# Low parts of a recurrent layer's input projection moved from GpSimd to VectorE, and its gates, scans, transposes and states made between weight blocks

## What is computed

```python
proj = h @ w_in                       # 1024 x 4096: q, fz, iv, g
q = silu(q);  v = iv
logf = log(lb + (1 - lb) * sigmoid(fz))
k = (1 - lb) * sigmoid(-fz)
b = cumsum(logf)                      # in chunks of 64 tokens; running sequences: of 4
scores = (q * exp(b - b_mid)) @ (k * exp(b_mid - b)).T     # causal, in the chunk
o = scores @ v + (q * exp(b)) @ S     # S: state at the chunk's start
S = exp(b_last) * S + (k * exp(b_last - b)).T @ v          # next chunk's state
out = (rmsnorm(o) * norm_w * silu(g)) @ w_out
```

## Time and profile before

| | us |
|---|---|
| median of 3 runs | 2119.61 |
| lowest and highest run | 2115.03, 2119.63 |
| span of the profiled execution | 2113.4 |
| from the first product of the projection to that of the head loop (1078.58 to 1219.45) | 140.9 |
| PE busy, whole span | 1857.5 |
| DVE, ACT, POOL busy, whole span | 1699.5, 1275.6, 588.8 |

### The profile page before, as it was taken

The page is one execution under the profiler, slowest core; times in us unless marked ns, Lnnn a source line. Parts: engine busy times, 40 slices in busy tenths (PEclk is TensorE's granted clock), DMA queues, the critical chain, the costliest instruction groups (busy, mean ns, idle before and its releaser), DMA issues. The chain is left out here.

```text
span 2113.4 us, 48775 instructions
## 1 busy us (share of the span) xinstructions
PE 1857.5 (88%) x17644; PEld 1607.3 (76%) x17644; DVE 1699.5 (80%) x3245; ACT 1275.6 (60%) x2621; POOL 588.8 (28%) x473
## 2 busy tenths in 40 slices
PE   1254889899999999999988877999999999999998
PEld 0243667788888888888866665778898898888887
DVE  8899568878889888879835596797889897887996
ACT  3532478666565556656578674886565655656554
POOL 6495057600000022213247501791000001221330
PEclk7555899999999999999999958999999999999999
DMA  2000334555556588889854204455555566888894
GB/s 89 26 1 2 125 111 151 164 185 177 173 178 206 172 290 299 304 271 331 311 202 146 90 11 179 141 168 181 173 182 173 173 211 220 300 300 278 313 331 163
DMA packets 107550, 396.30 MB, mean 188 GB/s; under 512 B 12976, under 2 KB 12976, under 8 KB 107056
## 3 DMA queue, kind: packets, MB, share of 16 engines
q1 hardware_dynamic: 88416, 318.37, 42.8%
q0 software_dynamic: 19024, 76.59, 11.8%
HBM read 388.72 MB, written 6.19 MB: 187 GB/s over the span
## 5 line engine op out<-in xcount | busy, mean ns | idle before, releaser
L229 ACT ACTIVATE wsp<-ring 128x512 f16<-128x512 f32 x1200 | 749.4, 629 | 627.4 <-PE ps L292 599.0
L290 PE MATMUL ps<-hs,wsp 128*128 128x256 f16 (+1 forms) x2672 | 737.9, 276 | 43.6 <-POOL wsp L240 31.5
L292 PE MATMUL ps<-hs,wsp 128*128 128x256 f16 (+1 forms) x2672 | 737.5, 276 | 0.0
L291 PE MATMUL ps<-hs,wsp 128*128 128x256 f16 (+1 forms) x2672 | 737.4, 276 | 0.0
L290 PE MATMUL ps<-hT,wsp 128*128 128x256 f16 x2048 | 559.1, 273 | 6.3 <-DVE hT L1791 6.3
L291 PE MATMUL ps<-hT,wsp 128*128 128x256 f16 x2048 | 559.0, 273 | 0.0
L292 PE MATMUL ps<-hT,wsp 128*128 128x256 f16 x2048 | 559.0, 273 | 0.0
L242 DVE SCALAR_TENSOR_TENSOR wsp<-ring,wsp 128x512 f16<-128x512 f32 x560 | 374.7, 690 | 134.3 <-ACT wsp L229 132.7
L249 DVE SCALAR_TENSOR_TENSOR wsp<-ring,wsp 128x1024 f16<-128x1024 f32 x216 | 264.2, 1224 | 102.9 <-ACT wsp L229 98.2
L290 PEld LDWEIGHTS ps<-hs,wsp 128*128 128x128 f16 x2672 | 261.6, 98 | 92.3 <-POOL wsp L240 34.0
L1550 POOL DMA_INDIRECT big<-in_rows,small x64 | 75.0, 1172 | 890.7 <-DVE small L1472 532.2
(11 more groups left out here) (299 smaller groups left out, 2110.2 us busy)
## 6 DMA issues: line engine op xcount, KB each, us to landing
ring<-in_v SPq DMA_DIRECT2D x256, 512.0 KB, 5.9
ring<-in_ub SPq DMA_DIRECT2D x216, 512.0 KB, 3.8
ring<-in_ua SPq DMA_DIRECT2D x40, 512.0 KB, 4.2
ring<-in_wq SPq DMA_DIRECT2D x32, 512.0 KB, 3.7
ring<-in_win SPq DMA_DIRECT2D x32, 512.0 KB, 3.7
ring<-in_glu SPq DMA_DIRECT2D x16, 512.0 KB, 4.3
big<-in_hgs POOLq DMA_DIRECT2D x1, 4096.0 KB, 13.3
ring<-in_wout SPq DMA_DIRECT2D x8, 512.0 KB, 3.9
```

The costliest lines, as they stand in the source:

```text
L229: nc.scalar.activation(wsp[:, k % 2, 0, cols], ring[:, k, cols], ACT.Copy, scale=scale).then_inc(hi_ready, 1)
L290: nc.tensor.matmul(out, w_hi, hi, start=start, stop=False, **kw)
L291: nc.tensor.matmul(out, w_hi, lo, start=False, stop=False, **kw)
L292: return nc.tensor.matmul(out, w_lo, hi, start=False, stop=stop, **kw)
```

## The change

1. "win" leaves `BY_POOL`: VectorE makes its low parts (line 242 in place of 240), the scaling pass of ScalarE is gone, GpSimd's loop over the 32 blocks too. The lows of block 0 are made at the end of peer_v_dve, those of block 1 in norm_dve between the rows of hT and their low parts.
2. The blocks come in the order fz, v, q, g. Q_ and D1 swap places in `big`. The first three heads of q are copied out and get their silu later in one operation.
3. The work on the gates is cut into pieces, each tied to a block number: a gate per head at blocks 1 to 8, two scans at each of 10 to 13, differences by half the heads at 14 to 17, products by half the heads at 19 to 25, 27 and 28. ScalarE's large activations stand at 8, 9, 14 and 16 to 19.
4. PE transposes the values behind blocks 23, 24, 25, the keys behind 25, 26, 27, and makes the chunk products behind 29, 30, 31. ScalarE copies the values out at blocks 24 to 26, VectorE the keys at 26 to 28; the chunk states stand right behind VectorE's loop, ahead of the masks.
5. The projection's trips are written out on PE (eight times four blocks) where a loop stood.
6. The lower bounds are worked out during the second pass of the expert layer ahead, at its blocks 66 and 71. Some semaphores of the expert layers are shared by both layers.

```diff
-BY_POOL = {"wq0", "ua0", "wq1", "ua1", "win"}
+BY_POOL = {"wq0", "ua0", "wq1", "ua1"}
...
+            if k == 2:
+                split_lo(v, "win", 0, 1)
             if before:
                 for c in range(KC):
                     low(c)
...
+                if L == 0 and b == 66:
+                    hg_lb_start_dve(v, cnt)
+                if L == 0 and b == 71:
+                    hg_lb_dve(v, cnt)
+            if L == 0:
+                split_lo(v, "win", 0, 0)
...
+        def hg_values_pe(pe, j):
+            pe.wait_ge(hg_ev, 16)
+            if j:
+                pe.wait_ge(hg_tvc, j)
+            hg_transpose_pe(pe, VT, 0, j, hg_tv)
+
+        def hg_keys_pe(pe, j):
+            pe.wait_ge(hg_m, 4)
+            if j:
+                pe.wait_ge(hg_tkc, j)
+            hg_transpose_pe(pe, KD, 2, j, hg_tk)
+
+        def hg_chunk_pe(pe, c):
+            pe.wait_ge(hg_tvc, 3)
+            pe.wait_ge(hg_tkc, 3)
+            if c >= 2:
+                pe.wait_ge(hg_S, c - 1)
...
         def hg_in_pe(pe):
-            project(pe, "win", lambda i, k, first: None if first else pe.wait_ge(hg_ev, i * 4 + k - 3),
-                    inputs=2)
+            def after(i, k, first):
+                b = i * RING + k
+                if 23 <= b < 26:
+                    hg_values_pe(pe, b - 23)
+                if 25 <= b < 28:
+                    hg_keys_pe(pe, b - 25)
+                if b >= 29:
+                    hg_chunk_pe(pe, b - 29)
+            for trip in range(8):
+                project(pe, "win", lambda i, k, first: None if first else pe.wait_ge(hg_ev, i * 4 + k - 3), after,
+                        trip, trip + 1, inputs=2)
+            hg_chunk_pe(pe, 3)
...
+            def between(b):
+                if b in (8, 9):
+                    heads_ = slice(4 * (b - 8), 4 * (b - 8) + 4)
+                    act.wait_ge(hg_f, 8 * (b - 7))
+                    nc.scalar.activation(h3(Bc)[:, heads_, :], h3(Bc)[:, heads_, :], ACT.Ln).then_inc(hg_log, 1)
+                elif b == 14:
+                    act.wait_ge(hg_cum, 8)
+                    nc.scalar.activation(QI, CU, ACT.Exp).then_inc(hg_e, 1)
+                elif b == 16:
+                    act.wait_ge(hg_d, 3)
+                    nc.scalar.activation(QM, D1, ACT.Exp).then_inc(hg_e, 1)
+                elif b == 17:
+                    nc.scalar.activation(KM, D1, ACT.Exp, scale=-1.0).then_inc(hg_e, 1)
+                elif b == 18:
+                    act.wait_ge(hg_d, 6)
+                    nc.scalar.activation(KD, Bc, ACT.Exp).then_inc(hg_e, 1)
+                elif b == 19:
+                    act.wait_ge(hg_ev, 16 + QUICK)
+                    nc.scalar.activation(h3(Q_)[:, 0:QUICK, :], h3(Q_)[:, 0:QUICK, :], ACT.Silu).then_inc(hg_e, 1)
+                elif 24 <= b < 27:
+                    hg_values_act(act, b - 24)
...
+            for b in range(32):
+                if b + 2 < 32:
+                    split_lo(v, "win", *divmod(b + 2, RING))
+                if 1 <= b < 9:
+                    gate(b - 1)
+                elif 10 <= b < 14:
+                    for h in (2 * (b - 10), 2 * (b - 10) + 1):
+                        scan(h)
...
+                if b in (24, 25):
+                    v.wait_ge(hg_ev, 24)
+                    v.wait_ge(hg_e, 5)
+                    times(QI, Q_, b - 24)
+                elif 26 <= b < 29:
+                    keys_out(b - 26)
+                if b in (27, 28):
+                    times(QM, Q_, b - 27)
...
+            for c in range(NCH):
+                state(c)
```

More of the change, by code:

```diff
@@ L1827, in h3 @@
             return a.rearrange("p (h t) -> p h t", h=HH)
-        Bc, K_, Q_, VT, GS, QM, QI, KM, KD, D1 = (unit(k) for k in range(10))
+        Bc, K_, D1, VT, GS, QM, QI, KM, KD, Q_ = (unit(k) for k in range(10))
         CU = bg(U * 10, U)
@@ L1856, in build @@
         lbr = sb("lbr", [P, 2, KC])
-        lb, oml = (small[:, 8 * k:8 * k + 8] for k in range(2))
-        lt = [small[:, 16 + 8 * k:24 + 8 * k] for k in range(4)]
+        lb, oml = (small[:, 200 + 8 * k:208 + 8 * k] for k in range(2))
+        lt = [small[:, 216 + 8 * k:224 + 8 * k] for k in range(4)]
         dec = small[:, 64:64 + 12 * HH].rearrange("p (h c) -> p h c", h=HH)
@@ new lines, in hg_values_pe @@
+        def hg_values_pe(pe, j):
[13 more added lines that the diff above has]
+                pe.wait_ge(hg_S, c - 1)
+            j, r0 = c // 2, CH * (c % 2)
+            for h in range(HH):
+                mm = nc.tensor.matmul(ps[:, 2 * (c % 2) + h // 4, (h % 4) * P:(h % 4 + 1) * P],
+                                      ktok[j][r0:r0 + CH, h * P:(h + 1) * P], vtok[j][r0:r0 + CH, h * P:(h + 1) * P],
+                                      start=True, stop=True)
+            mm.then_inc(hg_kv, 1)
@@ new lines, in build, with hg_evac_act @@
+        QUICK = 3
+        def hg_evac_act(act, b):
+            block_used(act, "win", *divmod(b, RING))
+            h = b % HH
+            if b < 8:
+                fns = [(Bc, ACT.Sigmoid, 1.0), (K_, ACT.Sigmoid, -1.0)]
+            elif b < 16:
+                fns = [(VT, ACT.Copy, 1.0)]
+            elif b < 24:
+                fns = [(Q_, ACT.Copy if h < QUICK else ACT.Silu, 1.0)]
+            else:
+                fns = [(GS, ACT.Silu, 1.0)]
+            for dst, fn, scale in fns:
+                ins = nc.scalar.activation(h3(dst)[:, h, :], zbank(b % RING), fn, scale=scale * UNSC)
+            ins.then_inc(hg_ev, 1)
@@ L1965, in hg_act, with hg_values_act @@
+        def hg_values_act(act, j):
+            w = TILES[j][1]
+            act.wait_ge(hg_tv, j + 1)
+            if j == 0:
+                act.wait_ge(hg_m, 4)
+            nc.scalar.activation(vtok[j][0:w, :], ps[0:w, 0:2, :].rearrange("p b n -> p (b n)"),
+                                 ACT.Copy).then_inc(hg_tvc, 1)
         def hg_act(act):
             act.wait_ge(x_ready, 2)
-            for trip in range(2):
-                hg_evac_act(act, trip, [(Bc, ACT.Sigmoid, 1.0), (K_, ACT.Sigmoid, -1.0)])
@@ L1991, in hg_act, with post @@
+            def post(i, k, first):
+                b = i * RING + k
+                hg_evac_act(act, b)
+                between(b)
+            for trip in range(8):
+                per_block(act, "win", split_hi, post, trip, trip + 1, ahead=2)
             act.wait_ge(hg_tvc, 3)
```

217 lines of the change are left out of this document (98 added, 119 removed).

## The result

| | us |
|---|---|
| median before, 4 runs | 2117.32 (2114.40 to 2119.63) |
| median of the changed kernel, 4 runs | 2102.89 (2100.16 to 2108.90) |
| ratio | 0.9947, 95% interval 0.9934 to 0.9960 |
| span of the profiled execution, before and changed | 2113.4 and 2107.2 |
| first product of the projection to that of the head loop, before and changed | 140.9 and 132.9 |

The change makes the kernel 0.53% faster; 2107.0 was forecast, with a range of 2097 to 2114.

A forecast was written before the change was run, and what follows sets the result against it. PE, busy 88% of the 2113.4 us span, was taken as the bound. The first output product moving 12.6 us earlier gives a span of 2100.8; with the median's 6.2 us distance kept, 2107.0 us, range 2097 to 2114.

The forecast's parts named there:

- 1. Start of the projection: Projection start: block 2 starts at 1088.5 instead of 1089.02, gaining 0.5 us; block 3 waits 0.15 us for ScalarE.
- 2. Pace of the blocks: Projection blocks 2 to 29 at PE's pace: 28 x 2.94 = 82.3 us, plus 0.4 booked, range 0 to 1.5.
- the lower prices: VectorE's costs in the projection from rows without GpSimd: scan 0.74 us, multiplication 2.6 for 2304 elements; no wait for PE.
- Rival A: VectorE becomes the projection's bound at prices measured beside GpSimd: 3 to 4 us of waiting, 2110.7 us; chance 0.15.
- the swallowed 3.0: In the projection blocks, 3.0 us of lag on VectorE or ScalarE is absorbed before PE stops.
- 3. The four waits: PE waits for copies of transposed values and keys behind blocks 24 to 27: 2 x 1.95 + 2 x 2.58 = 9.1 us.
- 4. States and head loop: Behind the blocks: states done at 1202.85, not 1219.35; first output product at 1206.8 in place of 1219.45, 12.6 us earlier.
- 5. The rest and the distance to the median: Outside the stage: lower-bound work 0, at most 1.3 us; span 2100.8, median's distance of 6.2 kept, giving 2107.0 us.
- Rival C: The new waits make PE's clock fall to 1.2 GHz, blocks 27 to 31 taking 5.9 us each: 2134 us; chance 0.06.
- Rival B: Larger gain: new waits hidden (2097.9 us), or PE's clock survives into the first heads (about 2104); chance 0.12 in all.
- Rival D: Something else paces the projection blocks (ScalarE's lag, written-out instruction stream or weight loads): 2113 to 2119 us; chance 0.09.

The follow-up runs named there:

- the spread kernel: Changed kernel with its transposes one group per block (values behind 23, 25, 27, keys behind 24, 26, 28), chunk products in pairs; 2090.78 and 2091.32 us, ratio 0.9887.

## Why the prediction held, step by step

**1. Start of the projection.** Predicted 0.5 us gained; it was 2.4. The normalized rows took 3.52 us for eight, where they had taken 5.03 with GpSimd at work (and take 5.03 again with GpSimd's lows back), so block 2 started 8.05 us behind the first product (1086.52 and 1078.47) and not 9.9. I had priced the lows that move here, but not what GpSimd's absence does to the rows that stay. 1.9 us too pessimistic.

**2. Pace of the blocks.** The choice of the lower prices was the one that mattered, and it was right: scan 740 ns (0.74 worked out), half multiplication 1348 (1.3 worked out), gate operations 423, 363 and 302. VectorE made PE wait once, 0.3 us; ScalarE's lag cost 0.4 behind it; 0.55 had been booked for both. The 0.74 came from the first layer's mean of 1307 ns for 512 columns, in which some scans took up to 2275; by their median of 1210 it would have been 0.68, so this fit is in part luck. Rival A is void; by its own terms its price was also too high, since 5.7 us less the swallowed 3.0 leave 2.7, not 3 to 4. In the experiment with GpSimd's lows the scan goes from 740 to 1192 ns. The Trainium skill's rule on the shared port (SBUF — State Buffer, "Who interferes with whom"), that a VectorE instruction with two SBUF inputs and a GpSimd instruction that reads SBUF lock each other out, agrees with that row. The rows also show that the number of tensors alone does not tell: the gate operations whose factors are read from `small`, one large input each, go from 423 to 914 and from 363 to 699 ns, the one with a constant stays (302 and 298).

**3. The four waits.** Predicted 1.95, 1.95, 2.58, 2.58; measured 2.02, 2.02, 2.67, 2.67, in all three profiles. Each is the chain that was added up: high half, evacuation or low half, copy. That nothing hides them is shown by the spread kernel, which is shorter by 9.9 us of stage for 9.4 us of waits.

**4. States and head loop.** Predicted: head loop 128.2 us behind the first product (1206.8 less 1078.58). Measured: 128.0 in the profiles of 2100.0 and 2100.1, 132.9 in that of 2108.9. So the stage is predicted to 0.2 us for executions with the clock up, in part by luck, as errors cancel: the start 1.9 to 2.1 too long, against 0.3 in the waits, 0.5 in the two lone chunk products (1.98 from start to start in place of 1.75), and by difference some 1.1 in short gaps between the blocks and behind them. The order of VectorE behind chunk product 2 and its length came as worked out: 1202.41 is the start of state 2 in the first profile, 1210.84 that of the queries' split, 1211.41 the head loop: 9.0 us, 8.9 worked out. One reading was wrong without bearing on the sum: the scores of the third tile were said to wait for the first masked copies "as before", but the earlier trace rows show all 48 scores in one piece (1203.57); that wait, 1.18 us, is new.

**5. The rest and the distance to the median.** The forecast of 2107.0 lies 4 us above the measured median and 6 above the common runs. The stage explains 12.9 us of the 15.1 between the spans 2113.4 and 2098.3; 1.7 us lie ahead of it and 0.5 behind, where such differences come and go between executions of one kernel (the first product lies between 1076.6 and 1081.6 in kernels that are alike up to there). The term mis-sized was the distance of 6.2 us from span to time. In the 37 executions of the kernel before, 33 took 2113.2 to 2115.5 us and four 2119.6 to 2119.7; two of those four were among the first three, hence the first median. A span of 2113.4 belonged to an execution of about 2115, as the changed kernel's 2098.3 and 2107.2 belong to 2100.0 and 2108.9: 1.7 us apart. By that distance the forecast would have been 2102.5. That this is near the first median, 2102.9, is chance again: two of those four executions were long ones, and the common ones lie at 2100 to 2101.

**Rival C**, the fall of the clock, had a chance of 0.06 and a price of 27 us. It did happen, in one of three profiles (whether in the other three long executions is open), and for 4.9 us, not 27. What failed there was to hold it for all or nothing: the clock came back while PE worked between the pauses (0.76, 0.97, 0.61, 0.82, 0.75, then 1.00 in stretches of 4 to 7 us from 1164 on). Slow were 24 transposes and some 19 of the 48 products of blocks 27 and 28, at 0.24 us from start to start in place of 0.12, and not five blocks.

**Rival B**, that the clock survives into the head loop, came in part and was worth little. Before, the clock was at 0.50 when the head loop began, and its first two products took 0.77 us. In the three profiles of the changed kernel they took 0.46, the clock was still at 1.00 in the 4 us ahead of them, and it was at 0.50 from 4 to 8 us behind their start. From the head loop's start to the end it is 893.4 us in the profiles of 2100.0 and 2100.1, 894.0 before and 895.8 in that of 2108.9. Rival D did not come either: between the blocks PE shows no wait but those named, and the rolled loop changes nothing.

The two halves of the change are told apart by four ratios. Lows on VectorE and gates in pieces, PE's tail as before: 0.9897. With PE's part moved as in the change: 0.9947. With that part moved, but a block between a transpose and its copy's use: 0.9887. All but the lows moved: 0.9983. So the gain is made by the lows and the gates together; moving the transposes and states gave back about half of it. A better place for them shortens the stage by 1.7 to 2.4 us (117.4 to 118.1 against 119.8), which the intervals of the ratios can't confirm. Two things were not run: the lows on VectorE with the gates uncut, so whether the cutting is needed is open, and GpSimd's lows with the transposes spread.

## What to carry to other kernels

Work put between the steps of a stream has to be followed to its consumer: here the copy that frees a bank stands, on its own engine, behind steps which only the end of the current block releases, so the next use of the bank must be a whole block away. Taking an engine off a stage also changes the price of what stays, so take durations from rows in which the same neighbours are at work. A pause of two microseconds on PE cost more than itself in one profile here and not in two others, so read more than one. And ask which execution a profiled span belongs to before adding a median's distance to it: that was the largest error of this forecast.

## What the runs showed of the hardware

- Pauses of 2.02 and 2.67 us with 3 to 4 us of work between them left PE's granted clock at 1.00 in two profiles and brought it down to 0.61 for 4 us in a third, with the same instructions. The Trainium skill (TensorE: Matmul & The Clock Gate, "What's actually happening") tells of a gate that follows recent activity. The profile with the fall agrees; here the same pauses tripped it once in three.
- A pause of 1.40 us behind transposes was followed by 0.50 through 19 us of products, though PE was then busy all the time (10.00 of 10.00 us from 1190 on, in the version with the chunk products ahead of the scores): 64 float32 products with 64 rows and 48 scores passed before the clock came back. In the version in which the scores follow the transposes without a pause it was at 1.00 up to 1190, until the last chunk products. Whether the pause or the work behind it decided was not separated.
- A float32 scan costs 740 ns for 288 columns when GpSimd is idle, 1192 to 1307 beside it. Of 512 columns it takes 1199 to 2275 in the first layer, the median 1210.
